# S5 kernel matrices from products of 32 stationary columns, and a final norm with tokens as rows

## The reference

```python
u = _rmsnorm(h, norm_g[layer])
# S5: 64 groups of 16 channels, 64 complex states each
ab = exp(dt * a)                        # complex, per group and state
bb = (ab - 1) / a * b                   # complex
x_t = ab * x_{t-1} + bb @ u_t           # scan over positions
y_t = Re(c @ x_t) + d_skip * u_t
...
h = h + mix @ w_out[layer]
...
return _rmsnorm(h, final_norm_g)[:, N_META:]   # y = h * rsqrt(mean(h*h) + eps) * g
```

## Time and profile before

| | |
|---|---|
| median of 3 runs | 1992.9 us (1989.21 to 1995.55) |
| the profiled execution | 1990.12 us |
| its span | 1988.3 us |
| PE busy | 1824.9 us (92%) |
| DVE busy | 980.3 us (49%) |
| ACT busy | 713.2 us (36%) |
| POOL busy | 781.4 us (39%) |
| mean granted TensorE clock | 0.953 |

### The profile page before, as it was taken

The page is one execution under the profiler, slowest core; times in us unless marked ns, Lnnn a source line. Parts: engine busy times, 40 slices in busy tenths (PEclk is TensorE's granted clock), DMA queues, the critical chain, the costliest instruction groups (busy, mean ns, idle before and its releaser), DMA issues.

```text
span 1988.3 us, 29697 instructions
## 1 busy us (share of the span) xinstructions
PE 1824.9 (92%) x12351; PEld 1636.7 (82%) x12351; DVE 980.3 (49%) x1565; ACT 713.2 (36%) x1271; POOL 781.4 (39%) x475
## 2 busy tenths in 40 slices
PE   6977899999988999879998999999999799899996
PEld 4977898899988999879997987777788688778884
DVE  7988124422428983277663132523333589634223
ACT  3354332444542222233333453333455222223321
POOL 2544565333223333333331586653332323334440
PEclk8988899899998999989999998999999999999998
DMA  8443336222254545524443332532222645443331
GB/s 146 124 148 123 102 86 139 70 75 73 56 129 145 176 139 118 145 69 139 132 129 93 104 96 83 110 107 80 67 72 70 166 167 185 107 133 102 94 94 56
DMA packets 349758, 221.27 MB, mean 111 GB/s; under 512 B 49589, under 2 KB 338537, under 8 KB 347065
## 3 DMA queue, kind: packets, MB, share of 16 engines
q1 hardware_dynamic: 347320, 189.75, 35.8%
q10 hardware_dynamic: 2304, 29.62, 4.0%
HBM read 171.65 MB, written 38.50 MB: 106 GB/s over the span
## 4 chain that ended last, share of the span: by engine, by line
PE 68%; DVE 14%; POOL 5%; DMA 5%; SPq 3%; ACT 2%; issue 2%; ACTq 0%; DVEq 0%; POOLq 0%
PE ring L756 51%; DMA sb_w_raw<-in_w_in 3%; PE ring L738 3%; POOL sb_w_lo L641 2%; PE aux L992 2%; DVE sb_s_mat_prod L1451 2%; PE aux L1084 1%; PE aux L1071 1%; SPq L555 1%; PE aux L805 1%; DVE sb_s_gelu_lo L1451 1%; DVE sb_s_prod L1451 1%; PE aux L1037 1%; PE aux L1013 1%; PE aux L781 1%
## 5 line engine op out<-in xcount | busy, mean ns | idle before, releaser
L641 POOL TENSOR_TENSOR sb_w_lo<-sb_w_raw,sb_w_hi 128x1024 fp32r<-128x1024 f32 x246 | 607.2, 2470 | 1107.0 <-ACT sb_w_hi L1143 1104.7
L1143 ACT ACTIVATE sb_w_hi<-sb_w_raw 128x1024 fp32r<-128x1024 f32 x246 | 259.8, 1057 | 636.3 <-DMA sb_w_raw<-in_w_in 421.4
L756 PE MATMUL ring<-sb_u_hi,sb_w_hi 128*128 128x264 f32 (+1 forms) x2144 | 366.4, 324 | 38.8 <-DVE sb_tmp_dve L1522 28.2
L756 PEld LDWEIGHTS ring<-sb_u_hi,sb_w_hi 128*128 128x128 f32 x2144 | 311.1, 197 | 71.6 <-DVE sb_tmp_dve L1522 29.7
L756 PE MATMUL ring<-sb_u_lo,sb_w_hi 128*128 128x264 f32 (+1 forms) x2144 | 346.9, 313 | 0.0
L756 PE MATMUL ring<-sb_u_hi,sb_w_lo 128*128 128x264 f32 (+1 forms) x2144 | 338.7, 308 | 0.0
L756 PEld LDWEIGHTS ring<-sb_u_lo,sb_w_hi 128*128 128x128 f32 x2144 | 306.6, 193 | 22.3
L756 PEld LDWEIGHTS ring<-sb_u_hi,sb_w_lo 128*128 128x128 f32 x2144 | 298.0, 188 | 21.1
L1175 ACT ACTIVATE sb_tmp_act<-ring 128x528 f32<-128x528 f32 (+1 forms) x112 | 67.5, 603 | 152.1 <-PE ring L756 139.3
L1381 ACT ACTIVATE sb_att_scores<-sb_att_scores,sb_att_neg_max 128x208 f32<-128x208 f32 x128 | 58.5, 458 | 93.9 <-DVE sb_att_neg_max L1741 93.9
L756 PE MATMUL ring<-sb_y_hi,sb_w_hi 128*128 128x264 f32 (+1 forms) x504 | 87.3, 322 | 0.0
(11 more groups left out here) (312 smaller groups left out, 2695.8 us busy)
## 6 DMA issues: line engine op xcount, KB each, us to landing
sb_w_raw<-in_w_in SPq DMA_DIRECT2D x166, 512.0 KB, 4.0
sb_s_loaded<-s_matrices ACTq DMA_DIRECT2D x16, 1808.0 KB, 7.3
s_matrices<-sb_s_phase SPq DMA_DIRECT2D x16, 528.0 KB, 3.2
s_matrices<-sb_s_mbt SPq DMA_DIRECT2D x16, 512.0 KB, 2.8
s_matrices<-sb_s_ca SPq DMA_DIRECT2D x16, 512.0 KB, 4.2
sb_w_raw<-in_w_gla_out SPq DMA_DIRECT2D x16, 512.0 KB, 3.9
sb_w_raw<-in_w_attn_out SPq DMA_DIRECT2D x16, 512.0 KB, 4.0
sb_w_raw<-in_s_w_glu SPq DMA_DIRECT2D x16, 512.0 KB, 4.0
```

Source lines behind the costliest of these rows:

```text
L641: pool.tensor_tensor(WL[:, w], WR[:, w], WH[:, w].bitcast(F32), ALU.subtract).then_inc(lo_ready, 1)
L756: last = pe.matmul(RING[:, 2 * r + hf, 0:c1 - c0], w[:, n % SLOTS, kt, :], moving(b[0], xx[:, kt], c0, c1), start=(term == 0 and kt == 0), ...
L1143: act.activation(WH[:, w], WR[:, w], ACT.Copy).then_inc(hi_ready, 1)
```

## The change

Toeplitz sums. The position groups of `toep` are shifted copies of one row: the product of the first piece of bbar with `cam` at distances 0 to 3. The change computes only that row. For each of four quads `q`, 32 stationary columns of `mbm` (its first piece) times 128 columns of `cam` give 32 output partitions, at partition 32q. One product of the identity with a `[128, 32]` diagonal adds the skip. `brep` and the repeated eye rows (`eyes`) are gone. ScalarE copies the result once, behind 96 columns that stay zero, and the spill makes the shifts: four stores, each of a window of 128 columns that begins 32 columns further on. What lies in DRAM afterwards is what lay there before.

Final norm. After each block `wout j` of the last layer TensorE turns column block `j-1` of the residual for all 512 tokens (`tokens_out`, four transposes). ScalarE squares it from PSUM (`token_squares`), VectorE multiplies it with the final scale, which is now loaded as rows (`FG`), and adds the squares per token (`tokens_in`). Behind the last block the sums, root and reciprocal are taken on `[128, 4]`, and VectorE and ScalarE scale two groups of 128 tokens each, which are then stored. The matrix-of-ones sum, the eight scalings and the PSUM copies behind the last block are gone.

Square root table. An operation on one element (`WARM`) is put ahead of each norm's squares, and ahead of the last block's squares in the final norm.

```diff
@@ PE step_matrices
-                for q in range(QUADS):
-                    for ri in range(2):
-                        last = pe.matmul(AX_[:, 2 * h, P * q:P * q + P],
-                                         MB[m]["brep"][:, ri, q].rearrange("p a b -> p (a b)"),
-                                         MB[m]["cam"][:, j % 2, ri, q, 0:4].rearrange("p a b -> p (a b)"),
-                                         start=(ri == 0), stop=(ri == 1))
-                        if ri == 0:
-                            pe.matmul(AX_[:, 2 * h, P * q:P * q + 32],
-                                      MB[m]["eyes"][:].rearrange("p a b -> p (a b)"),
-                                      MB[m]["dsk"][:, 32 * q:32 * q + 32],
-                                      start=False, stop=False)
+                for ri in range(2):
+                    for q in range(QUADS):
+                        pe.matmul(AX_[32 * q:32 * q + 32, 2 * h, 0:P], mbm[:, ri, q, 0],
+                                  cam[:, ri, q, 0:4].rearrange("p a b -> p (a b)"),
+                                  start=(ri == 0), stop=False)
+                pe.matmul(AX_[:, 2 * h, 0:32], ID[:], MB[m]["dsk"][:], start=False, stop=True
+                          ).then_inc(aux_full[h], 1)
@@ ACT matrices_out
-                for p in range(STRIDE):
-                    rows = slice(32 * p, 32 * p + 32)
-                    last = act.activation(
-                        MB[m]["toep"][rows, :, STRIDE - 1 - p:STRIDE],
...
+                act.activation(MB[m]["toep"][:, 3 * 32:], AX_[:, 2 * h, 0:P], ACT.Copy
+                               ).then_inc(aux_free[h], 1)
@@ SP spill_mats
-                sp.dma_start(mat_part(d, "toep"), MB[m]["toep"][:].rearrange("p q t i -> p (q t i)")
-                             ).then_inc(mats_spilled[j % 2], 16)
+                for p in range(STRIDE):
+                    sp.dma_start(mat_part(d, "toep")[32 * p:32 * p + 32].rearrange("i (q x) -> q i x", q=QUADS),
+                                 MB[m]["toep"][:, 32 * p:32 * p + P]).then_inc(mats_spilled[j % 2], 16)
@@ DVE s5_matrices
-                dve.tensor_scalar(MB[m]["dsk"][:], ID[:], SD[:, m, j:j + 1], None, ALU.mult)
-                for ri in range(2):
-                    last = dve.tensor_copy(BREP[:, ri], MBM[:, ri, :, 0:1].broadcast_to([P, QUADS, 4, 32]))
-                link(last)
+                link(dve.tensor_scalar(MB[m]["dsk"][:], EYE32[:], SD[:, m, j:j + 1], None, ALU.mult))
@@ DVE input_matrix
-                dve.tensor_copy(MB[m]["eyes"][:], EYE32[:].unsqueeze(1).broadcast_to([P, 4, 32]))
@@ PE, final norm; called behind each block wout j of the last layer, for j - 1
+            def tokens_out(j):
+                evacuated(pe, DEPTH - 1, ("wout", j))
+                h = aux_take(1, ("fin", j))
+                for t in range(SEQ // P):
+                    last = pe.transpose(AX_[:, 2 * h, P * t:P * t + P],
+                                        H[:, j, N_META + P * t:N_META + P * t + P], ID[:])
+                last.then_inc(aux_full[h], 1)
@@ ACT, final norm, and the table
+            def token_squares(j):
+                h = aux_result(act, 1, ("fin", j))
+                if j >= 2:
+                    act.wait_ge(fin_ready, j - 1)
+                act.activation(FSQ[:, j % 2].rearrange("p t d -> p (t d)"), AX_[:, 2 * h], ACT.Square
+                               ).then_inc(fsq_ready, 1)
+            for ly in range(DEPTH):
+                link(act.activation(WARM[:, 0:1], ONES[:, 0:1], ACT.Sqrt))
...
+            link(act.activation(WARM[:, 0:1], ONES[:, 0:1], ACT.Sqrt))
+            token_squares(KT - 1)
+            act.wait_ge(fvar_ready, 1)
+            act.activation(FV[:, 1], FV[:, 0], ACT.Sqrt).then_inc(fstd_ready, 1)
+            act.wait_ge(frs_ready, 1)
+            for t in (2, 3):
+                act.activation(XO[:, t], XO[:, t], ACT.Copy, scale=FV[:, 0, t:t + 1]).then_inc(out_ready[1], 1)
@@ DVE, final norm
+            def tokens_in(j):
+                if j == 0:
+                    dve.wait_ge(fg_loaded, 16)
+                h = aux_result(dve, 1, ("fin", j))
+                dve.wait_ge(fsq_ready, j + 1)
+                tt(XO[:, :, P * j:P * j + P], AX_[:, 2 * h].rearrange("p (t d) -> p t d", d=P),
+                   FG[:, P * j:P * j + P].unsqueeze(1).broadcast_to([P, 4, P]), ALU.mult).then_inc(aux_free[h], 1)
+                link(dve.reduce_sum(FSS[:, :, j], FSQ[:, j % 2], AX.X))
...
+            for t in (0, 1):
+                dve.tensor_scalar(XO[:, t], XO[:, t], FV[:, 0, t:t + 1], None, ALU.mult).then_inc(out_ready[0], 1)
@@ SP, after all blocks
+            for i in range(2):
+                for e in range(2):
+                    t = 2 * e + i
+                    sp.wait_ge(out_ready[e], i + 1)
+                    sp.dma_start(out[0, P * t:P * t + P, :], XO[:, t]).then_inc(out_stored, 16)
```

More of the change, by code:

```diff
@@ L1118, in _ @@
                     mat_turn(ly, ("wout", j))
[L1120 to L1128 removed]
+                    if ly == DEPTH - 1:
+                        tokens_out(j - 1)
+            tokens_out(KT - 1)
         @block.scalar
```

100 lines of the change are left out of this document (42 added, 58 removed).

## The result

The changed kernel takes 1959.35 us (median of 4 runs, 1954.82 to 1961.96), the kernel before 1991.69 us in the same comparison: a ratio of 0.9833, 95% interval 0.9808 to 0.9859, or 32.3 us less. The forecast was 1962.0 us, with 28.9 us saved. The profiled execution is the fastest of the four, 1954.8 us with a span of 1953.0.

A forecast was written before the change was run, and what follows sets the result against it. TensorE carries 68% of the chain, so savings pay only where it waits, plus the serial tail. 11.4 + 5.3 - 1.2 + 13.4 = 28.9 us saved; forecast 1962 us, range 1949 to 1975.

The forecast's parts named there:

- Toeplitz products: S5 steps on TensorE: 1.4 us warm, 2.8 at half clock; saves 1.3 us a step, bounds 0.4 and 1.9.
- the rival of four products at once: S5 products on TensorE: four quarters overlap fully, 0.6 us less on seven steps, 1958 us; chance 0.08.
- VectorE: S5 steps: two wide copies gone (0.68 us) and a smaller diagonal save 0.77 us a step; GpSimd's stall not counted saved.
- stalls are freed too: Rival: VectorE's stalls beside GpSimd fall into its wait for TensorE, 6.6 us more plus 2 in second stage, 1953; chance 0.12.
- First stage: Layer 0's S5 matrices: three cycles give 8.6 us, steps 0 and 1 give 2.8; sum 11.4, bounds 5 and 18.
- SyncE at nothing: Spill's four Toeplitz stores land net 0 to 2 us later, with 5 us to spare until VectorE is ready; cost nothing.
- The sign named as wrong: In the spill: ScalarE's transposes copy waiting several microseconds for the Toeplitz stores would show the forecast wrong.
- the spill takes over: Rival: small stores land one after another, 4.5 us each; some 65 us lost against 29 won, 2026; chance 0.03.
- Second stage: S5 matrices from 870 us: first step 1.1, next 0.3, four nothing, steps 5 to 7 3 x 1.3; 5.3, bounds 1 and 11.
- Layer norm of layer 1: Square-root table load ahead of the squares makes TensorE start later: cost 1.2 us.
- Tail: After last projection: 30.0 us becomes 13.9, less 2.7 for transposes between projections; 13.4 saved, bounds 10 and 15.
- a change of tiling mode drains the engine: Skill's rule for S5 products: two added changes a step, guessed 0.2 us each on seven steps, 2.8 us less; not counted.

The follow-up runs named there:

- the two parts: Kernel before with only the S5 (Toeplitz) edit, 1971.31 us; changed kernel with the S5 part as before, 1975.97 us.
- the norm part alone: Changed kernel with the S5 part as before, leaving the final norm and earlier table load in the layer norms: 1975.97 us, ratio 0.9926.
- The two experiments that undo a part: Changed kernel with VectorE's two spreading copies put back, 1960.87 us; changed kernel with all eight products on the same 32 TensorE columns, 1964.29 us.
- two buffers: Changed kernel with kernel-matrix tiles double-buffered by step parity, so ScalarE need not wait for the last step's stores: 1959.51 us, ratio 0.9844.
- changed kernel's second trace: Changed kernel run once more, unaltered, in the comparison with the split-tail kernel: 1960.54 us, ratio 0.9868.
- an earlier load: Changed kernel with ScalarE's square-root table load moved ahead, to before each layer's attention output projection: 1959.82 us, ratio 0.9851.

## Why the prediction was right, and where it was not

The sum was 28.9 us; the medians give 32.3 and the two parts 31.8. By its own steps:

- **Toeplitz products**, taken at 1.4 us at the full clock and 2.8 at half of it (warm and cold in what follows), from the attention's rows of 64 columns. They take 0.91 and 1.59. This is the term that was mis-sized: the rival of four products at once was true, and I had given it 0.08. The choice of the nearest row held the error, as it shows two groups and here are four. The products on the path of the first stage come after a wait, begin at the lower clock, and took 4.2 us there. They save 2.6, not the 1.3 that the cycle was charged with; by the forecast's own cold figure it would have been 4.2 - 2.8 = 1.4, so the rate and not the clock is the error. By VectorE's lost waits (7.2 to 0.4) and the last turn (2.5), the products are worth 9.3 us of the first stage, where the forecast has 4 x 1.3 = 5.2.
- **VectorE**, 0.77 us in each of eight steps, 6.2 us. Measured 5.9 us less busy time in the eight steps; the copies alone, put back, cost 5.4. Right. That GpSimd's stall is not saved but falls on the next instruction held too: each of the three cycles still has the stall of some 2 us that stood on the copies (the row at 135.16). The rival "stalls are freed too" is answered by this.
- **First stage** in sum: 11.4 forecast, 17.1 measured, inside the bounds of 5 to 18. The three cycles, between the ends of the odd steps' products, take 22.5, 22.9 and 27.2 us, where 26.4, 27.3 and 30.8 stood: 11.9 us less for 8.6 forecast. The forecast's 24.4 us for each took all three for alike. Steps 0 and 1 give 5.2 for 2.8, and 2.1 of that is VectorE's earlier start, which the forecast does not have. The start differs between kernels (77.4 to 78.3 us in seven other traces, the norm part alone among them, whose stage still ends at 199.6), so how much of it is the change's stays open. The two experiments that undo a part add up to 11.8 (5.4 + 6.4). The other 5.3 were not undone separately. That start and the four small products with the identity (0.31 us each) belong to them; what else is open.
- **SyncE at nothing.** Right in the sum, wrong in the cover. The prediction saw 5 us to spare; the spill's landing is level with VectorE's chain within 0.4 us. The sign named as wrong, ScalarE waiting several microseconds for the Toeplitz stores, came true (4.3 us in three waits), but it told little, as ScalarE waited 3.1 us in two before the change as well. It costs nothing because VectorE ends no earlier (two buffers: 182.3). The rival "the spill takes over" named a price per store that no row had. The price is the issue, 3.7 us for four where one took 1.0: from ScalarE's copy to the landing it was 5.8 us and is 8.6 (109.87 to 118.43). By its own terms, seven steps at 7.1 and seven at 3.7 to 5.7, that rival would also have lost 76 us or more, not 65.
- **Second stage**: 5.3 forecast, 5.2 in the profiled execution and 2.5 in the changed kernel's second trace. So it is luck that 5.3 was met so closely. The last two steps bear their part in every trace: 15.3 us apart before, 13.8 on average now, 1.5 a step where 1.3 was taken. In the profiled execution they give 2.9 us and not three times 1.3, since step 5 comes no earlier behind step 4 (33.7 us in both). Step 0 gives 3.4 where 1.1 was forecast, and steps 2 and 3 lose 1.9. Whether VectorE's copies are worth their part in the first steps is not shown.
- **Layer norm of layer 1**: 1.2 forecast, 1.7 measured as TensorE's wait (1.8 in the table for the norm part), and taken back by an earlier load.
- **Tail**: from the last projection 13.9 forecast, 13.4 measured; so 16.6 saved there. The 2.7 us for the transposes between the projections can't be read off one trace. From the norm's first sum to the last projection's end the two kernels without transposes take 895.0 and 894.9 us, the twelve with them 893.7 to 900.2, in the middle 897.1: some 2 us, within a spread of 6.5.

So the forecast was close to the time with a true mechanism and a term too small on the safe side: 5.7 us too little in the first stage, 0.5 too little cost in the norm. That the medians moved by 32.3 and not by some 34 is within the spread, and the second stage is the part that varies most. The last step from 28.9 us to 1962 took off 2.0 us without a reason, as 28.9 below the median of 1992.9 is 1964.0; beside an effect that was too small it happened to help. The rule of the Trainium skill (TensorEngine Tiling, "Key Properties") that a change of tiling mode drains the engine was to cost 2.8 us at my guess. The trace shows less. Start to start, step 7's transposes take 0.96 us (1023.06 to 1024.02), those of step 6 in the kernel before 0.87 (1027.06 to 1027.93); the small product 0.24 until the projection goes on (1024.60 to 1024.84), before 0.14 (1028.16 to 1028.30). That is 0.1 us on either side of the 32-column products, whatever its cause, and half of my guess. The same page's "Theoretical Speedup", up to 4x at 32 columns, is met at 3.2 to 3.3 by this trace.

## What to carry to other kernels

Where products have few stationary columns, price them from a row with as many groups as they will have, and at the clock that TensorE has after the wait on which they stand. Where VectorE never idles in a stage, count its operations by their undisturbed durations: a long mean beside GpSimd's work is a stall that moves on. When a transfer is cut in four, the issue on its queue is the price. The cover is the time between its landing and each engine that waits for it, the one two steps on as well (here VectorE, 0.4 us), not the wait seen before; doubling the stores shows in one run how little is left of it.

## What the runs showed that I had not expected

Four groups of 32 columns overlap whatever the order: two products on the same group back to back (0.67 us for 16 passes) cost no more than the groups in turn (0.64), where one group alone takes 1.93. A chain of waits that runs through a spill (4.5 to 5.1 us of landing at each step) was no bound: with that wait taken away the stage ended at the same 182.3 us, as a second chain was level with it.
